# Splitting each 512-column up product of the experts into two products of 256 columns

## The chip, the cores and the metric

The program runs on one core of a Trainium2 chip, in one launch. The metric is the device time of one execution in microseconds (us). TensorE (PE in the rows) multiplies; its weight loads, which bring the stationary operand into the array, have rows of their own (PEld). VectorE is DVE, ScalarE is ACT, GpSimd is POOL, and SyncE (SP) issues nearly all DMAs.

## The reference

Two blocks follow each other, each of two layers over 256 tokens of 1024 features. Only the last part of the second block, a mixture of experts, is touched here:

```
D_MODEL, SEQ, N_EXPERTS, TOP_K, EXPERT_DIM = 1024, 256, 8, 2, 3584

def moe_swiglu(x, w_router, w_gate, w_up, w_down):
    xf = x.reshape(bsz * t, d)
    logits = (xf @ w_router).astype(jnp.float32)
    top_val, top_idx = lax.top_k(logits, TOP_K)
    top_w = jax.nn.softmax(top_val, axis=-1)
    gates = jnp.einsum('nk,nke->ne', top_w, jax.nn.one_hot(top_idx, N_EXPERTS, dtype=jnp.float32))
    out = jnp.zeros_like(xf)
    for e in range(N_EXPERTS):
        h = jax.nn.silu(xf @ w_gate[e]) * (xf @ w_up[e])
        out = out + gates[:, e:e + 1].astype(xf.dtype) * (h @ w_down[e])
    return out.reshape(bsz, t, d)
```

Before it stand the first block (three kinds of attention and an MLP, twice), a gated delta net, a dense SwiGLU of width 2816 (called ffn below) and a window attention.

## The kernel before

All of it is written by hand, engine by engine: in every stage each engine has its own program, its instructions run in the order in which they are written, and engines wait for each other on semaphores.

The part of the experts works on 8 experts of 14 steps each, so 112 steps. A step has 256 hidden columns. Its weights come as three units of 1 MB (128 partitions by 2048 numbers): two "up" units, each with four chunks of 128 input rows and 512 columns (256 of the gate beside 256 of the up matrix), and one "down" unit of two chunks by 1024 columns. That makes 336 units. `moe_order` puts them in order: the two up units of step i, then the down unit of step i - 2 (`LAG`).

Float32 accuracy is made of three products with operands of type float32r. ScalarE rounds a unit into `moe_high` (L3368), VectorE subtracts it from the raw unit to get `moe_low` (L3408), and the tokens of the expert (128 places, gathered) have `moe_xh` and `moe_xl` likewise. TensorE multiplies high by high, high by low and low by high. There are four buffers for split units (`UNITS`), and seven places for raw ones, six in the tile `ring` and one in `xT`. SyncE loads unit u + 7 when VectorE has made unit u's low part (`ring.load`, L3013).

For an up unit the stationary operand is a 128 by 128 block of the tokens, the moving operand one chunk of the unit with its 512 columns, and the result fills one bank of PSUM: gate in columns 0 to 255, up in columns 256 to 511. Four chunks by three kinds of product by two units make 24 products a step (L3312), 2688 in all, which accumulate in one bank for each step. The down products (L3318, 12 a step, 1344 in all) also have 512 columns. After the second up unit of a step TensorE transposes the hidden values of the step before (L3329). ScalarE's SiLU (L3378) and VectorE's product (L3417) read the bank only when all 24 products of the step have ended. At some steps TensorE also gathers tokens for later experts (L3082: moving operand `moe_pick` with 256 columns, stationary blocks of `moe_x_high` or `moe_x_low`) or spreads an expert's result (L3098, L3099: four products of 512 columns in a row with the same stationary block of `moe_pickT`).

Other stages use the same kind of product with 256 moving columns: the ffn's up products (L2023, where the tokens move and 128 by 128 blocks of weights are stationary) and projections (L927).

Of the kernel before, what the change touches and what calls it, by code (L numbers as in the profile page):

```python
# [68 lines left out]
FB = 256  # L69
# [2972 lines left out]
def place(m):  # L3042

    return (0, 1, 0, 2)[m % 4]
# [15 lines left out]
def turn_pick(pe, core, r, m, s, banks):  # L3060

    pick = r["pick"].bitcast(F32)
    for k in range(2):
        for t in range(NT):
            pe.transpose(banks[0][0:CAP, (k * NT + t) * P:(k * NT + t + 1) * P], pick[:, t, k, :], core.const("ident"))
    for k in range(2):
        for t in range(NT):
            mm = pe.matmul(banks[1][0:CAP, k:k + 1], pick[:, t, k, :], r["gates"][:, t, m + k:m + k + 1],
                           start=(t == 0), stop=(t == NT - 1))
    mm.then_inc(s["pick_turned"], 1)  # L3070
# [7 lines left out]
def gather(pe, r, x, chunks, banks):  # L3078

    for n, c in enumerate(chunks):  # L3080
        for t in range(NT):
            mm = pe.matmul(banks[n // 2][:, (n % 2) * 2 * CAP:(n % 2 + 1) * 2 * CAP], x[:, t, c * P:(c + 1) * P],  # L3082
                           r["pick"][:, t, :, :].rearrange("p k n -> p (k n)"), start=(t == 0), stop=(t == NT - 1))
    return mm
# [8 lines left out]
def spread(pe, r, m, t, banks):  # L3093

    for half in range(2):
        cols = slice(half * BANK, (half + 1) * BANK)
        turned = r["pickT"][:, place(m), t * P:(t + 1) * P]
        pe.matmul(banks[half][:], turned, r["yh"][:, cols], start=True, stop=False)  # L3098
        mm = pe.matmul(banks[half][:], turned, r["yl"][:, cols], start=False, stop=True)  # L3099
    return mm  # L3100
# [154 lines left out]
def expert_stage(core, ring, order, r, s):  # L3255
# [3 lines left out]
    high, low, xh, xl, hh, hl, sg = (r[n] for n in ("high", "low", "xh", "xl", "hh", "hl", "sg"))  # L3259
# [10 lines left out]
    def unit(buffers, u):  # L3270
        return unit_of(buffers, ring, u)

    def wait_split(eng, name, u):

        if u >= AHEAD:
            eng.wait_ge(s[name], u - AHEAD + 1)
# [7 lines left out]
    with nc.Block() as block:  # L3284
        @block.sync
        def _(sp):
            for u in range(n_units):
                wait_split(sp, "weight_low", u)
                ring.load(sp, u + len(ring.places))

        @block.tensor
        def _(pe):
            for u, (kind, i, part) in enumerate(order):
                m, own = divmod(i, STEPS)
                wait_split(pe, "weight_high", u)
                if kind == "up" and part == 0 and i >= 2:
                    pe.wait_ge(s["product"], i - 1)
                if kind == "up" and part == 0 and own == 0 and m and m % 2 == 0:
                    pe.wait_ge(s["x_high"], 2 * m)
                    pe.wait_ge(s["x_low"], 2 * m)  # L3300
                if kind == "down":
                    pe.wait_ge(s["hidden_low"], i + 1)
                    if own == 0 and m:
                        pe.wait_ge(s["y_high"], 2 * m)
                        pe.wait_ge(s["y_low"], 2 * m)
                for j, (buffer, other_low) in enumerate(((high, False), (high, True), (low, False))):
                    wt = unit(buffer, u)
                    if j == 2:
                        wait_split(pe, "weight_low", u)
                    if kind == "up":  # L3310
                        for c in range(4):
                            mm = pe.matmul(core.banks[i % 2][:], (xl if other_low else xh)[:, place(m), 4 * part + c, :],  # L3312
                                           wt[:, c, :], start=(part == 0 and j == 0 and c == 0),
                                           stop=(part == 1 and j == 2 and c == 3))
                    else:
                        for half in range(2):
                            for c in range(2):
                                mm = pe.matmul(core.banks[4 + half][:], (hl if other_low else hh)[:, i % 2, c, :],  # L3318
                                               wt[:, c, half * BANK:(half + 1) * BANK],
                                               start=(own == 0 and j == 0 and c == 0),  # L3320
                                               stop=(own == STEPS - 1 and j == 2 and c == 1))
                mm.then_inc(s["unit_used"], 1)
                if u in turn_after:
                    k = turn_after[u]
                    pe.wait_ge(s["product"], k + 1)
                    if k >= 2:
                        pe.wait_ge(s["hidden_low"], k - 1)
                    for c in range(2):
                        mm = pe.transpose(core.banks[2 + k % 2][:, c * CAP:(c + 1) * CAP],  # L3329
                                          sg[:, k % 2, c * P:(c + 1) * P], core.const("ident"))  # L3330
                    mm.then_inc(s["turned"], 1)
                if kind != "up" or part != 1:
                    continue
                if own in SPREAD and m:
                    t = SPREAD.index(own)
                    if t:
                        pe.wait_ge(s["added"], 4 * (m - 1) + 2)
                    else:
                        pe.wait_ge(s["y_high"], 2 * m)
                        pe.wait_ge(s["y_low"], 2 * m)  # L3340
                    spread(pe, r, m - 1, t, core.banks[6:8]).then_inc(s["spread"], 1)
                if own == TURN and m % 2 == 0:
                    pe.wait_ge(s["added"], 4 * m)
                    turn_pick(pe, core, r, m, s, core.banks[6:8])
                if own in GATHER and m % 2:
                    n = GATHER.index(own)
                    pairs = (m - 1) // 2
                    if n == 0:
                        pe.wait_ge(s["picked"], 2 * (pairs + 1))
                        pe.wait_ge(s["added"], 4 * m)  # L3350
                    else:
                        pe.wait_ge(s["x_high"], 4 * pairs + n)
                        pe.wait_ge(s["x_low"], 4 * pairs + n)
                    for rows, bank in ((r["x_high"], 6), (r["x_low"], 7)):
                        gather(pe, r, rows, range(2 * n, 2 * n + 2), core.banks[bank:bank + 1]).then_inc(s["gathered"], 1)
            pe.wait_ge(s["y_high"], 2 * E)
            pe.wait_ge(s["y_low"], 2 * E)
            for t in range(NT):
                spread(pe, r, E - 1, t, core.banks[2 * t:2 * t + 2]).then_inc(s["spread"], 1)
# [310 lines left out]
```

## Time and profile before

| | |
|---|---|
| device time of three runs | 2519.05, 2517.83, 2513.12 us (median 2517.83) |
| span of the profiled execution | 2513.8 us, mean granted TensorE clock 0.985 |
| TensorE busy over the span | 2411.1 us, 96% |
| VectorE, ScalarE busy | 1750.4 us (70%), 1416.7 us (56%) |
| loop over the experts' steps | 1511.3 us to about 2493.7 us of the span |

The profile gives no device time of the profiled execution besides its span, so its own time is taken as 2513.8 us; it lies within the three runs, 4.0 us under their median.

A product's row in the timeline has a start and a duration. Products overlap in the array, so a duration (390 ns for 512 columns) is longer than the distance from one start to the next, and what a product costs in a stream is that distance.

### The profile page before, as it was taken

Reading aid. Unit: us, or ns where it says so; the run is one execution under the profiler, and the core shown is the slowest. Engines: PE = TensorE matmul, PEld = TensorE weight load, DVE = VectorE, ACT = ScalarE, POOL = GpSimd, SP = SyncE. Lnnn points to the kernel's source line nnn. Section 1 sums busy time; section 2 is a strip of 40 time slices with the busy share of each in tenths; the row PEclk is TensorE's granted clock in tenths of the full one; section 3 lists DMA queues with packets and bytes.
Section 4 is the critical chain, followed back from the end, with each engine's and each line's share of the span. In section 5 each row is a group of like instructions: output and inputs, shape, how many; then the busy total and the mean of one; then the engine's idle time right before and its main releaser. Section 6 shows DMA issues by size and latency. Waiting matters only on the chain. (4 is left out here: it accounts for less than half of the span.)

```text
span 2513.8 us, 34646 instructions
## 1 busy us (share of the span) xinstructions
PE 2411.1 (96%) x13815; PEld 2050.2 (82%) x13815; DVE 1750.4 (70%) x2026; ACT 1416.7 (56%) x1624; POOL 136.5 (5%) x176
## 2 busy tenths in 40 slices
PE   6999999999998999998999999999999999999997
PEld 6797789888777898787998888888888888888885
DVE  3357655544676555576545678898899888888987
ACT  4544544453454445433434547777777777777775
POOL 0102200000121000060000000000000000000000
PEclk9999999999999999899999989999999999999998
DMA  8243455533345555405556249999999999999997
GB/s 290 103 140 133 157 188 185 191 135 111 132 151 182 180 198 142 96 1 187 179 188 209 86 134 340 367 366 364 359 363 360 357 354 366 361 356 351 366 362 244
DMA packets 391568, 586.59 MB, mean 233 GB/s; under 512 B 21168, under 2 KB 284656, under 8 KB 391280
## 3 DMA queue, kind: packets, MB, share of 16 engines
q1 hardware_dynamic: 391408, 584.38, 68.7%
q8 instruction: 110, 1.80, 0.3%
q14 instruction: 50, 0.41, 0.1%
HBM read 580.14 MB, written 4.19 MB: 232 GB/s over the span
## 5 line engine op out<-in xcount | busy, mean ns | idle before, releaser
L3408 DVE TENSOR_TENSOR moe_low<-ring,moe_high 128x2048 fp32r<-128x2048 f32 x288 | 658.8, 2290 | 94.2 <-ACT moe_high L3368 90.8
L3368 ACT CAST moe_high<-ring 128x2048 fp32r<-128x2048 f32 x288 | 548.9, 1909 | 143.9 <-PE bank L3312 72.6
L3312 PE MATMUL bank<-moe_high,moe_xh 128*128 128x512 f32 x896 | 243.2, 393 | 1.0 <-PEq L3147 1.0
L3312 PE MATMUL bank<-moe_low,moe_xh 128*128 128x512 f32 x896 | 241.3, 391 | 0.0
L3312 PE MATMUL bank<-moe_high,moe_xl 128*128 128x512 f32 x896 | 240.7, 390 | 0.0
L3312 PEld LDWEIGHTS bank<-moe_high,moe_xh 128*128 128x128 f32 x896 | 168.0, 188 | 38.0 <-issue 1.1
L3312 PEld LDWEIGHTS bank<-moe_high,moe_xl 128*128 128x128 f32 x896 | 168.2, 188 | 37.1
L3312 PEld LDWEIGHTS bank<-moe_low,moe_xh 128*128 128x128 f32 x896 | 168.2, 188 | 37.1
L2079 DVE TENSOR_TENSOR chain_low<-ring,chain_high 128x2048 fp32r<-128x2048 f32 x48 | 110.0, 2292 | 115.7 <-ACT chain_high L2052 115.7
L2052 ACT CAST chain_high<-ring 128x2048 fp32r<-128x2048 f32 x44 | 84.2, 1913 | 139.9 <-PE bank L2023 106.0
L3318 PE MATMUL bank<-moe_high,moe_hh 128*128 128x512 f32 x448 | 128.5, 408 | 0.0
L3318 PE MATMUL bank<-moe_low,moe_hh 128*128 128x512 f32 x448 | 120.6, 391 | 0.0
L3318 PE MATMUL bank<-moe_high,moe_hl 128*128 128x512 f32 x448 | 120.4, 391 | 0.0
L3408 DVE TENSOR_TENSOR moe_low<-xT,moe_high 128x2048 fp32r<-128x2048 f32 x48 | 110.0, 2291 | 13.9 <-ACT moe_high L3368 13.4
L3368 ACT CAST moe_high<-xT 128x2048 fp32r<-128x2048 f32 x48 | 91.6, 1909 | 26.9 <-PE bank L3312 14.0
L2079 DVE TENSOR_TENSOR chain_ffn_low<-ring,chain_ffn_high 128x2048 fp32r<-128x2048 f32 (+1 forms) x34 | 65.0, 1913 | 58.4 <-ACT chain_ffn_high L2052 58.4
L3318 PEld LDWEIGHTS bank<-moe_high,moe_hl 128*128 128x128 f32 x448 | 84.1, 188 | 18.8
L3318 PEld LDWEIGHTS bank<-moe_low,moe_hh 128*128 128x128 f32 x448 | 84.1, 188 | 18.6
L3378 ACT ACTIVATE consts<-bank 128x256 f32<-128x256 f32 x112 | 43.1, 385 | 86.5 <-PE bank L3312 86.5
L2052 ACT CAST chain_ffn_high<-ring 128x2048 fp32r<-128x2048 f32 (+1 forms) x32 | 50.9, 1590 | 66.5 <-PE bank L2023 45.5
L3318 PEld LDWEIGHTS bank<-moe_high,moe_hh 128*128 128x128 f32 x448 | 76.8, 189 | 11.0 <-issue 0.2
L967 DVE TENSOR_TENSOR chain_low<-ring,chain_high 128x1024 fp32r<-128x1024 f32 x36 | 44.0, 1224 | 44.3 <-ACT chain_high L952 35.1
(518 smaller groups left out, 4860.4 us busy)
## 6 DMA issues: line engine op xcount, KB each, us to landing
ring<-in_moe_w_gate SPq DMA_DIRECT2D x199, 512.0 KB, 5.5
ring<-in_moe_w_up SPq DMA_DIRECT2D x199, 512.0 KB, 7.1
ring<-in_moe_w_down SPq DMA_DIRECT2D x95, 1024.0 KB, 7.5
ring<-in_w_in SPq DMA_DIRECT2D x22, 2048.0 KB, 8.1
ring<-in_w_down SPq DMA_DIRECT2D x14, 2048.0 KB, 7.8
ring<-in_w_up SPq DMA_DIRECT2D x10, 2048.0 KB, 8.1
xT<-in_moe_w_down SPq DMA_DIRECT2D x18, 1024.0 KB, 7.5
xT<-in_moe_w_gate SPq DMA_DIRECT2D x31, 512.0 KB, 5.5
```

The lines of the kernel that those rows point to most:

```text
L967: dve.tensor_tensor(unit(core.low, u), raw(u), unit(core.high, u), ALU.subtract)\
L2052: act.copy(unit(core.high, u), raw(u)).then_inc(s["weight_high"], 1)
L2079: dve.tensor_tensor(unit(core.low, u), raw(u), unit(core.high, u), ALU.subtract)\
L3312: mm = pe.matmul(core.banks[i % 2][:], (xl if other_low else xh)[:, place(m), 4 * part + c, :], wt[:, c, :], start=(part == 0 and j == 0 a ...
L3318: mm = pe.matmul(core.banks[4 + half][:], (hl if other_low else hh)[:, i % 2, c, :], wt[:, c, half * BANK:(half + 1) * BANK], start=(own = ...
L3368: act.copy(unit(high, u), ring.raw(u)).then_inc(s["weight_high"], 1)
L3378: act.activation(sg[:, i % 2, :], core.banks[i % 2][:, 0:FB], ACT.Silu).then_inc(s["silu"], 1)
L3408: dve.tensor_tensor(unit(low, u), ring.raw(u), unit(high, u), ALU.subtract)\
```

## The change

Each up product is issued as two: the first multiplies the stationary block by columns 0 to 255 of the chunk into columns 0 to 255 of the bank, the second the same stationary block by columns 256 to 511 into the other half. The flag that begins the accumulation stands on the first of the two alone, at the step's first chunk, and the one that ends it on the second at the step's last chunk. Nothing else changes.

```
--- before.py
+++ after.py
@@ -3309,9 +3309,11 @@
                         wait_split(pe, "weight_low", u)
                     if kind == "up":
                         for c in range(4):
-                            mm = pe.matmul(core.banks[i % 2][:], (xl if other_low else xh)[:, place(m), 4 * part + c, :],
-                                           wt[:, c, :], start=(part == 0 and j == 0 and c == 0),
-                                           stop=(part == 1 and j == 2 and c == 3))
+                            for side in range(2):
+                                cols = slice(side * FB, (side + 1) * FB)
+                                mm = pe.matmul(core.banks[i % 2][:, cols], (xl if other_low else xh)[:, place(m), 4 * part + c, :],
+                                               wt[:, c, cols], start=(part == 0 and j == 0 and c == 0 and side == 0),
+                                               stop=(part == 1 and j == 2 and c == 3 and side == 1))
                     else:
                         for half in range(2):
                             for c in range(2):
```

On TensorE one step with a gather stands in the program before like this (output, moving operand, stationary operand; columns; count):

```order
L3312 MATMUL bank<-moe_high,moe_xh 128x512 x4
L3312 MATMUL bank<-moe_high,moe_xl 128x512 x4
L3312 MATMUL bank<-moe_low,moe_xh 128x512 x4
L3312 MATMUL bank<-moe_high,moe_xh 128x512 x4
L3312 MATMUL bank<-moe_high,moe_xl 128x512 x4
L3312 MATMUL bank<-moe_low,moe_xh 128x512 x4
L3329 MATMUL bank<-consts 128x128 x2
L3082 MATMUL bank<-moe_pick,moe_x_high 128x256 x4
L3082 MATMUL bank<-moe_pick,moe_x_low 128x256 x4
L3318 MATMUL bank<-moe_high,moe_hh 128x512 x4
L3318 MATMUL bank<-moe_high,moe_hl 128x512 x4
L3318 MATMUL bank<-moe_low,moe_hh 128x512 x4
```

At the same place in the changed program TensorE has:

```order
L3314 MATMUL bank<-moe_high,moe_xh 128x256 x8
L3314 MATMUL bank<-moe_high,moe_xl 128x256 x8
L3314 MATMUL bank<-moe_low,moe_xh 128x256 x8
L3314 MATMUL bank<-moe_high,moe_xh 128x256 x8
L3314 MATMUL bank<-moe_high,moe_xl 128x256 x8
L3314 MATMUL bank<-moe_low,moe_xh 128x256 x8
L3331 MATMUL bank<-consts 128x128 x2
L3082 MATMUL bank<-moe_pick,moe_x_high 128x256 x4
L3082 MATMUL bank<-moe_pick,moe_x_low 128x256 x4
L3320 MATMUL bank<-moe_high,moe_hh 128x512 x4
L3320 MATMUL bank<-moe_high,moe_hl 128x512 x4
L3320 MATMUL bank<-moe_low,moe_hh 128x512 x4
```

Every group of four up products has become one of eight with half the columns; order, transposes, gathers and down products stand where they stood, two lines lower in the file.

## Rows read from the trace of the kernel before

**Rows 1.** The page's first part: span, and busy time of each engine.

```profile
span 2513.8 us, 34646 instructions
PE 2411.1 (96%) x13815; PEld 2050.2 (82%) x13815; DVE 1750.4 (70%) x2026; ACT 1416.7 (56%) x1624; POOL 136.5 (5%) x176
```

**Rows 2.** Busy time in one stretch of the experts' loop: its length, engines, clock, DMA.

```profile
1520.00:2490.00 970.00, 970.00 (x4438) 797.08 (x4437) 865.57 (x622) 711.58 (x593) 0.00 (x0) 1.00 1.06 361
```

**Rows 3.** Costliest groups of the page (busy, mean ns, idle before, releaser).

```profile
L3408 DVE TENSOR_TENSOR moe_low<-ring,moe_high 128x2048 fp32r<-128x2048 f32 x288 | 658.8, 2290 | 94.2 <-ACT moe_high L3368 90.8
L3368 ACT CAST moe_high<-ring 128x2048 fp32r<-128x2048 f32 x288 | 548.9, 1909 | 143.9 <-PE bank L3312 72.6
L3312 PE MATMUL bank<-moe_high,moe_xh 128*128 128x512 f32 x896 | 243.2, 393 | 1.0 <-PEq L3147 1.0
```

**Rows 4.** Timeline of the loop, all engines: start us, us, engine, line.

```profile
1995.66 2.29 DVE L3408 TENSOR_TENSOR moe_low<-ring,moe_high 128x2048 fp32r<-128x2048 f32 x1 [0.25 <-ACT moe_high L3368]
...
1998.74 1.91 ACT L3368 CAST moe_high<-ring 128x2048 fp32r<-128x2048 f32 x1 [0.84 <-PE bank L3312]
```

**Rows 5.** DMA in 1520 to 2490 us: queues (packets, MB, share); issues, us to landing.

```profile
q8 instruction: 36, 0.59, 0.3%
...
ring<-in_moe_w_down SPq DMA_DIRECT2D x94, 1024.0 KB, 7.5
```

**Rows 6.** TensorE's timeline in the loop, 512 columns: four steps in a row.

```profile
1608.64 1.09 PE L3312 MATMUL bank<-moe_high,moe_xh 128*128 128x512 f32 x4
...
1614.13 0.38 PE L3329 MATMUL bank<-consts 128*128 128x128 f32 x2
...
1617.11 1.08 PE L3312 MATMUL bank<-moe_high,moe_xh 128*128 128x512 f32 x4
...
1622.63 0.38 PE L3329 MATMUL bank<-consts 128*128 128x128 f32 x2
...
1625.62 1.10 PE L3312 MATMUL bank<-moe_high,moe_xh 128*128 128x512 f32 x4
...
1631.14 0.38 PE L3329 MATMUL bank<-consts 128*128 128x128 f32 x2
...
1634.09 1.07 PE L3312 MATMUL bank<-moe_high,moe_xh 128*128 128x512 f32 x4
...
1635.90 1.07 PE L3312 MATMUL bank<-moe_low,moe_xh 128*128 128x512 f32 x4
1636.81 1.10 PE L3312 MATMUL bank<-moe_high,moe_xh 128*128 128x512 f32 x4
...
1639.58 0.38 PE L3329 MATMUL bank<-consts 128*128 128x128 f32 x2
```

**Rows 7.** TensorE's timeline in the ffn: 96 products of 256 columns.

```profile
1272.94 1.10 PE L2023 MATMUL bank<-x_high,chain_ffn_high 128*128 128x256 f32 x8
1273.88 1.11 PE L2023 MATMUL bank<-x_low,chain_ffn_high 128*128 128x256 f32 x8
...
1275.78 1.07 PE L2023 MATMUL bank<-x_high,chain_ffn_high 128*128 128x256 f32 x8
...
1283.94 0.62 PE L2033 MATMUL bank<-chain_ffn_high,mlp_hh 128*128 128x512 f32 x2
```

**Rows 8.** TensorE's timeline in a projection: 84 products of 256 columns.

```profile
629.82 0.62 PE L927 MATMUL bank<-attention_high,x_high 128*128 128x256 f32 x4
...
639.34 0.38 PE L1461 MATMUL bank<-consts,lower_arena 128*72 128x128 f32 x2
```

**Rows 9.** TensorE's timeline at two gathers inside the experts' loop.

```profile
1684.45 0.62 PE L3082 MATMUL bank<-moe_pick,moe_x_low 128*128 128x256 f32 x4
1684.90 1.08 PE L3318 MATMUL bank<-moe_high,moe_hh 128*128 128x512 f32 x4
...
1702.34 0.64 PE L3082 MATMUL bank<-moe_pick,moe_x_low 128*128 128x256 f32 x4
1702.81 1.09 PE L3318 MATMUL bank<-moe_high,moe_hh 128*128 128x512 f32 x4
```

**Rows 10.** The spreading products' loads and products: duration ns min/median/max.

```profile
L3098 PEld LDWEIGHTS bank<-moe_yh,moe_pickT x32: 186/188/330, 1648.1 to 2497.9; 128*128 128x128 f32 x32
L3098 PE MATMUL bank<-moe_yh,moe_pickT x32: 393/476/628, 1648.2 to 2498.4; 128*128 128x512 f32 x32
```

**Rows 11.** TensorE's timeline at one spread in the loop, stationary block unchanged.

```profile
1648.48 0.40 PE L3099 MATMUL bank<-moe_yl,moe_pickT 128*128 128x512 f32 x1
...
1649.19 1.08 PE L3318 MATMUL bank<-moe_high,moe_hh 128*128 128x512 f32 x4
```

## The prediction, made before the changed kernel was run

> **What bounds the kernel now.** The page's first part shows TensorE busy for 96% of the span [rows 1]. The change touches the experts' loop alone, so the second view is that stretch: in 970 us TensorE is busy for all 970.00, at a granted clock of 1.00, beside VectorE at 865.57 and ScalarE at 711.58 [rows 2]. The costliest groups say who waits for whom: VectorE idles for ScalarE, ScalarE for TensorE (it needs the unit's buffer back), TensorE for nothing but 1.0 us at the loop's entry [rows 3]. So in the loop what sets the time is the distance from one product's start to the next, and the other engines follow.
>
> Two things could stop TensorE from being the limit if its pace changed. Weights: ScalarE's cast at 1998.74 stood idle until TensorE freed the buffer; it lasts 1.91 us, VectorE's subtraction of such a unit 2.29 us [rows 4], and a buffer comes back only every four units, nearly 12 us at about 3 us a unit. That leaves several us between a low part and its first use. DMA: the loop moves 361 GB/s [rows 2], a 1 MB unit lands 7.5 us after its issue [rows 5] and its place is loaded seven units, some 20 us, ahead. I read that as DMA being ahead, since ScalarE's waits name TensorE and no landing [rows 3].
>
> **The change, term by term.** It removes 2688 products of 512 columns and adds 5376 of 256, each with its own load of the stationary block. Nothing moves past anything, no wait is added, no DMA, no work on another engine. The last of the 24 products of a step, for which SiLU waits, becomes two; what both cost is in the term below. So the sum has one term: 2688 times (two paces at 256 columns less one pace at 512).
>
> *The pace at 512 columns.* Four steps in a row, after which the pattern of buffers repeats, have 24 products in 5.49, 5.52, 5.52 and 5.49 us: 22.02 / 96 = 229.4 ns [rows 6]. It isn't one level. The 12 products from 1634.09 to 1636.81 take 2.72 / 12 = 226.7 ns each, the others up to some 231.
>
> *The pace at 256 columns.* The loop has hardly any, but other places have many of the same type, each with a load of its own. In the ffn 96 take 11.00 us, 114.6 ns each; the first 24 of them, right behind products of 512 columns, take 2.84 / 24 = 118.3, and the other 72 take 8.16 / 72 = 113.3 [rows 7]. In a projection 84 take 9.52 us, again 113.3 [rows 8]. Inside the experts' loop, with VectorE, ScalarE and DMA as busy as they will be here, one gather has 0.45 / 4 = 112.5 ns and the next 0.47 / 4 = 117.5 [rows 9]. So there are two levels as well: 113.3 and about 117.5.
>
> The fast level is exactly half of the fast level at 512 (2 x 113.3 = 226.6 against 226.7): time goes by columns, and no fixed cost for a product shows. The slow level costs 8.4 ns a pair more.
>
> *The second load of the same block.* A load is issued for each product even where the block stays: the spreading products have 32 loads for 32 products [rows 10], and three in a row with an unchanged block take 0.71 / 3 = 237 ns [rows 11], near the slow level at 512 and no worse than two slow halves. Loading the same rows again is thus neither skipped nor dear, and at 256 columns the load fits beside the product in 113.3 ns.
>
> *Bounds and value.* All fast: 226.6 - 229.4 = -2.8 ns, -7.5 us. The ffn's mix: 229.2, -0.5 us. Half fast, half slow as in the gathers: 230.8, +3.8 us. All slow: 235.0, +15.1 us (with the ffn's 118.3 it would be +19.4). I take 115.0 ns, four in ten slow, between the ffn's stretch and the gathers, since each step here goes from 512 columns into 48 of 256, as the ffn goes into 96: 230.0 - 229.4 = +0.6 ns, times 2688 = **+1.6 us**. Against the profiled execution that is 2513.8 + 1.6 = 2515.4 us; carried over to the median of the runs, 4.0 us higher, it is 2517.8 + 1.6, about **2519 us**. A measurement of this kernel tells about 0.3% from no change, 7.5 us; the forecast is within it.
>
> A rule speaks against the change: the Trainium skill, "TensorE: Matmul & The Clock Gate", section "Back-to-back issue gap", gives a warm product N / 2.4 ns and a fixed 2.5 ns. By it a pair would cost 2.5 ns more than one product, +6.7 us. The rows of the fast level don't show that fixed part, 226.6 against 226.7.
>
> **Rivals.**
> *Slower, the slow level throughout.* Each up stretch follows products of 512 columns, the ffn's first 24 products behind such were slow [rows 7], and one gather of two never left the slow level [rows 9]. Here the stream switches every 48 products, and each unit begins on another buffer. At 117.5 ns a product: +15.1 us, 2533 us. It decides from a mean of 116.1 ns on (232.2 for a pair, 2.8 above today, 7.5 us). Against it: 72 of 96 in the ffn and all 84 in the projection are fast.
> *A fixed cost for each product.* Rows bound it for a pair between nothing (the fast level) and 235.0 - 229.4 = 5.6 ns (all of the slow level's excess, were it such a cost); the middle, 2.8 ns, is +7.5 us, 2525 us. The fast rows speak against it, the gather at 117.5 ns for it. The skill's fixed part, above, would be this rival.
> *Faster, the fast level throughout.* -7.5 us, 2510 us. For it: the projection, and that today's 512 columns are the ones that lose 2.7 ns to a slow level. It just touches the bound. If the second load were dropped, rows give no more than this, since the columns alone take 0.443 ns each at either width.
> *Code fetch.* TensorE's instructions come in packets: 36 for 4438 products and 4437 loads, if all are its own [rows 2, 5], so 5376 more instructions need some 22 more. A packet takes 0.3% of 970 us x 16 engines / 36 = 1.3 us; were TensorE to stand for each, +28 us, 2546 us. Today it stands for none [rows 2].
> *The change isn't what it says.* The order on TensorE shows eight products of 256 for each four of 512, so it is.
>
> **How the numbers follow.** Mix of levels, as forecast: 0.52. Slow throughout: 0.21. Fixed cost: 0.08. Fast throughout: 0.15. Code fetch: 0.04. Faster by over 0.3% is under half of the fast case, 0.07; slower is slow, fetch, and a little of the fixed cost and the mix's upper end, 0.29; within 0.3% the rest, 0.64. The range goes from the fast end, 2510, to the slow end, 2534; it leaves out the fetch stall and the outer halves of both ends' scatter, under 2 in 10. The likeliest case's own range is 2512 to 2525.
>
> **What would show it.** Right: groups of eight up products start 0.91 to 0.94 us apart; loads as many as products; TensorE busy all 970 us with no new releaser; ScalarE still waits for TensorE; the 12 down products as before. Wrong: up products at 117 ns or more each in most steps (slow rival); holes of about 1 us at regular distances of some 15 us (fetch); a TensorE wait on `moe_high` or `moe_low` (weights late after all); pairs whose second half starts sooner than 110 ns after the first (the load dropped or free). The prediction fails above all if the share of slow products is not that of the ffn, which depends on what stands around them.

## The result: slower by 0.8%, outside the predicted range

| | before | after |
|---|---|---|
| median of the runs | 2518.44 us | 2538.99 us |
| lowest and highest | 2513.12, 2520.42 us | 2534.37, 2540.62 us |
| span of the profiled execution | 2513.8 us | 2537.9 us |

The ratio of after to before is 1.0084, 95% interval 1.0071 to 1.0096. The medians are 20.5 us apart, the spans 24.1 us. Of these 24.1 us, 22.1 lie in the experts' loop, from the start of its first up product to that of its last product (982.0 us before, 1004.1 after). The range had ended at 2534 us, and no change was called likeliest.

The page of the changed kernel, its first part, the queue that carries code, and the three groups that answer to [rows 3]:

```profile
span 2537.9 us, 40022 instructions
...
PE 2435.5 (96%) x16503; PEld 2189.9 (86%) x16503; DVE 1751.7 (69%) x2026; ACT 1416.5 (56%) x1624; POOL 136.5 (5%) x176
...
q8 instruction: 131, 2.15, 0.4%
...
L3410 DVE TENSOR_TENSOR moe_low<-ring,moe_high 128x2048 fp32r<-128x2048 f32 x288 | 659.0, 2291 | 111.6 <-ACT moe_high L3370 106.7
L3370 ACT CAST moe_high<-ring 128x2048 fp32r<-128x2048 f32 x288 | 548.7, 1909 | 152.3 <-PE bank L3314 80.8
L3314 PE MATMUL bank<-moe_high,moe_xh 128*128 128x256 f32 x1792 | 248.8, 281 | 1.0 <-PEq L3147 1.0
```

TensorE's busy time has grown by 24.4 us, as much as the span. VectorE and ScalarE do the same work and idle more, for the same releasers as before. TensorE still waits for nothing but the 1.0 us at the entry. The stretch of [rows 2] in the changed kernel (length; TensorE, its loads, VectorE, ScalarE, GpSimd; clock; DMA share; GB/s):

```profile
1520.00:2490.00 970.00, 970.00 (x6943) 913.75 (x6942) 848.36 (x608) 694.79 (x578) 0.00 (x0) 1.00 1.03 354
```

TensorE is busy for all 970.00 us at the clock of before, and the other engines get less done in the same time (608 instructions on VectorE for 622, 354 GB/s for 361). So nothing stops TensorE: its products themselves come at a slower pace. The timeline of four steps in a row, which answers to [rows 6]:

```profile
1605.08 1.11 PE L3314 MATMUL bank<-moe_high,moe_xh 128*128 128x256 f32 x8
...
1610.78 0.38 PE L3331 MATMUL bank<-consts 128*128 128x128 f32 x2
...
1613.76 1.12 PE L3314 MATMUL bank<-moe_high,moe_xh 128*128 128x256 f32 x8
...
1619.52 0.38 PE L3331 MATMUL bank<-consts 128*128 128x128 f32 x2
...
1622.50 1.07 PE L3314 MATMUL bank<-moe_high,moe_xh 128*128 128x256 f32 x8
...
1625.22 1.12 PE L3314 MATMUL bank<-moe_high,moe_xh 128*128 128x256 f32 x8
...
1628.10 0.38 PE L3331 MATMUL bank<-consts 128*128 128x128 f32 x2
...
1631.08 1.11 PE L3314 MATMUL bank<-moe_high,moe_xh 128*128 128x256 f32 x8
...
1636.74 0.38 PE L3331 MATMUL bank<-consts 128*128 128x128 f32 x2
```

The four steps take 5.70, 5.76, 5.60 and 5.66 us, together 22.72 us for 192 products: 118.3 ns each, 236.7 for a pair against 229.4 before. That is +7.3 ns, and times 2688 it is +19.6 us, nearly the whole loss between the medians (20.5). Over the whole loop, added up in the trace from the start of each of the 224 up units to the start of what follows it, the up products take 616.3 us before and 637.7 us after, +21.4 us; the down products take 317.4 and 318.1 us.

There are three levels (a level is a pace that a stream of products holds), not the two that the prediction knew, and they go with the buffer of the weights. Units take the four buffers in turn, so these eight up units use buffers 3, 0, 2, 3, 1, 2, 0 and 1. Buffers 2 and 3 go at 120.0 ns (5.76 / 48 from 1613.76; 2.88 / 24 from 1625.22). Buffers 0 and 1 go at 117.9 (5.66 / 48 from 1631.08), once at 113.3 (2.72 / 24 from 1622.50). In the whole loop the 111 units in buffers 2 and 3 all settle at 120, and of the 113 units in buffers 0 and 1, 99 settle at 118 and 14 at 113. No row used for the prediction was above 118.3.

### The profile page after: what moved, and what is told of

It is laid out like the page before. It is cut to its first block and busy times, and to the rows that moved or that the text cites. A ratio compares the mean times of both kernels' runs of the same rounds, so it can differ in the third digit from the quotient of the medians.

```text
span 2537.9 us, 40022 instructions
## 1 busy us (share of the span) xinstructions
PE 2435.5 (96%) x16503; PEld 2189.9 (86%) x16503; DVE 1751.7 (69%) x2026; ACT 1416.5 (56%) x1624; POOL 136.5 (5%) x176
## 5 line engine op out<-in xcount | busy, mean ns | idle before, releaser
L3314 PE MATMUL bank<-moe_high,moe_xh 128*128 128x256 f32 x1792 | 248.8, 281 | 1.0 <-PEq L3147 1.0
L3314 PE MATMUL bank<-moe_low,moe_xh 128*128 128x256 f32 x1792 | 249.2, 281 | 0.0
L3314 PE MATMUL bank<-moe_high,moe_xl 128*128 128x256 f32 x1792 | 249.0, 281 | 0.0
L3314 PEld LDWEIGHTS bank<-moe_high,moe_xh 128*128 128x128 f32 x1792 | 235.6, 189 | 10.0 <-issue 1.1
L3314 PEld LDWEIGHTS bank<-moe_low,moe_xh 128*128 128x128 f32 x1792 | 228.5, 190 | 0.0
L3314 PEld LDWEIGHTS bank<-moe_high,moe_xl 128*128 128x128 f32 x1792 | 228.4, 190 | 0.0
```

What stands on the lines that cost most here:

```text
L3314: mm = pe.matmul(core.banks[i % 2][:, cols], (xl if other_low else xh)[:, place(m), 4 * part + c, :], wt[:, c, cols], start=(part == 0 and ...
```

## The experiments

Two theories stood at first. By A the loss is in what the split adds, the same block loaded twice in a row or halves of a bank that change with every product. By B it is in what the products read, since the levels differ by buffer and not by order. "The kernel" below is the changed one where not said otherwise; ratios are to the kernel before, with the 95% interval behind them.

**The halves in another order.** The first four products of a group go to one half, the next four to the other, so no block is loaded twice in a row and the half changes once:

```
...
-                        for c in range(4):
-                            for side in range(2):
+                        for side in range(2):
+                            for c in range(4):
...
```

> As the changed kernel, 5376 up products of 256 columns, but the four chunks run inside the two halves: no stationary block is loaded twice in a row, and the half of the bank stays for four products. Theory A (the second load of the block just loaded, or the change of half in the bank, costs some 5 ns a product): the mean distance of up products falls from 118.6 ns to 113 to 115 ns, the time to about 2512 to 2520 us, ratio to the kernel before 0.997 to 1.002. Theory B (any product of 256 columns with its own load costs this here, whatever the order): distance 118 to 120 ns, time about 2539 us, ratio 1.007 to 1.010.

Measured: 2541.81 us, ratio 1.0087 [1.0057, 1.0117], with the levels of the changed kernel, unit for unit (120 in buffers 2 and 3, 118 and 14 times 113 in the others); the up products add up to 637.7 us as there.

**Halves change, blocks don't repeat.**

```
...
+                        for turn in range(2):
+                            for c in range(4):
+                                side = (c + turn) % 2
...
```

> As the run before, but the halves of the bank alternate from product to product while the stationary block is another each time. If repeated loading of one block is the cost (theory A1): about 113 to 115 ns a product, ratio 0.997 to 1.002. If the alternation of the halves is the cost (theory A2), or theory B: 118 to 120 ns, ratio 1.007 to 1.010.

Measured: 2539.37 us, ratio 1.0082 [1.0054, 1.0111]. The same levels again, 638.0 us of up products.

**Blocks repeat, halves don't change.** The block of `moe_xh` is loaded for the high part and again for the low part, into one half:

```
...
+                    for side in range(2):
+                        cols = slice(side * FB, (side + 1) * FB)
+                        for c in range(4):
+                            for wt in (wh, wl):
+                                pe.matmul(bank[:, cols], xh[:, place(m), 4 * part + c, :], wt[:, c, cols],
...
```

> Products of 256 columns; the block of the tokens' high part is loaded twice in a row, for the unit's high and then its low part, and both products go into the same half of the bank; a third of the products (the tokens' low part) have another block each time. Theory A1 (repeated block costs): the first two thirds stay at 118 to 120 ns, the last third falls to about 113 ns, ratio about 1.005. Theory A2 (alternation costs): all at 113 to 115 ns, ratio 0.997 to 1.002. Theory B: all at 118 to 120 ns, ratio 1.007 to 1.010.

Measured: 2540.57 us, ratio 1.0087 [1.0057, 1.0116]. Its up products take 638.0 us. Four orders, with the repeated load or without and with the halves changing or not, give 1.0082 to 1.0087 and the same time of up products within 0.3 us. Theory A falls. The second load of a block costs what any load costs. A small kernel that was to run these orders with TensorE alone gave no result.

**The addresses alone.** What differs between buffers 0 and 1 and buffers 2 and 3 is where they lie: in the program's address map, in bytes within a partition and modulo 256 (the residue), the first two are at 224 and the other two at 160, as are the tokens' blocks `moe_xh` and `moe_xl`. No trace shows an address. That the blocks and buffers 2 and 3 agree follows from the sizes of the tiles between them, all multiples of 256 bytes; the 224 is the author's reading of the map, and the runs with gaps below bear it out. A small kernel of its own has streams of 96 products of 256 columns and of 24 of 512, with stationary tiles at 160 and 224 and moving tiles at each multiple of 32:

```
STAT = {"stat_e": 224, "stat_c": 160}
MOVE = {"mov_a": 0, "mov_b": 32, "mov_c": 64, "mov_d": 96, "mov_e": 128, "mov_f": 160, "mov_g": 192, "mov_h": 224}
...
                for x in STAT:
                    for w in MOVE:
                        narrow(pe, banks[0][:], stat[x], move[w])
                        wide(pe, banks[1][:], stat[x], move[w])
```

> A small kernel with none of the reference's computation. TensorE alone runs, for two stationary tiles (address 224 and 160 modulo 256, as the blocks of weights in the ffn and the experts' tokens have it) and eight moving tiles (addresses 0, 32, ... 224 modulo 256), 96 products of 256 columns and then 24 of 512; then four of these pairs again beside ScalarE's casts and VectorE's subtractions. In the experts' loop moving buffers at 160 (as the tokens) stood at 120.0 ns, those at 224 at 116.7 to 118. Theory C (the load and the moving reads collide by address): with equal residues 120 ns, with others 113.3 or 117.7, alone as well as beside the others. Theory D (the other engines' traffic does it): 113.3 throughout while TensorE is alone, 117 to 120 beside them. Theory E (a phase that the stream happens to lock into): levels of 113.3 and 117.7 without order by address, perhaps changing inside a group or kept from the group before.

Its timeline on TensorE (moving, stationary operand), the streams at the distances 64, 192 and 0 for the one stationary tile and then for the other:

```profile
65.38 11.04 PE L23 MATMUL bank<-mov_b,stat_e 128*128 128x256 f32 x96
76.25 5.66 PE L31 MATMUL bank<-mov_b,stat_e 128*128 128x512 f32 x24
...
132.87 11.06 PE L23 MATMUL bank<-mov_f,stat_e 128*128 128x256 f32 x96
143.76 5.76 PE L31 MATMUL bank<-mov_f,stat_e 128*128 128x512 f32 x24
...
166.31 11.67 PE L23 MATMUL bank<-mov_h,stat_e 128*128 128x256 f32 x96
177.82 5.63 PE L31 MATMUL bank<-mov_h,stat_e 128*128 128x512 f32 x24
183.28 11.67 PE L23 MATMUL bank<-mov_a,stat_c 128*128 128x256 f32 x96
...
267.84 11.67 PE L23 MATMUL bank<-mov_f,stat_c 128*128 128x256 f32 x96
279.35 5.63 PE L31 MATMUL bank<-mov_f,stat_c 128*128 128x512 f32 x24
284.82 11.36 PE L23 MATMUL bank<-mov_g,stat_c 128*128 128x256 f32 x96
...
301.62 11.04 PE L23 MATMUL bank<-mov_h,stat_c 128*128 128x256 f32 x96
312.50 5.66 PE L31 MATMUL bank<-mov_h,stat_c 128*128 128x512 f32 x24
317.99 0.22 PE L88 MATMUL bank<-stat_c 128*128 128x128 f32 x1
```

A stream's pace is the distance to the next stream's start over its count. With both operands at the same residue the 96 narrow products take 11.51 us (119.9 ns), for `stat_e` from 166.31 as for `stat_c` from 267.84. At 64 apart they take 10.87 and 10.88 us (113.3), from 65.38 and 301.62. So the single addresses don't matter, and the distance from the stationary to the moving operand does. By the sizes of its tiles the two pairs at distance 0 lie 66048 and 45312 bytes apart, which are 0 and 256 modulo 512, and they have the same pace, so a period of 512 isn't seen. All of them, as (start to start) / count, mean of the two tiles:

| moving less stationary, mod 256 | 0 | 32 | 64 | 96 | 128 | 160 | 192 | 224 |
|---|---|---|---|---|---|---|---|---|
| 256 columns, ns | 119.9 | 116.7 | 113.3 | 119.9 | 120.0 | 117.4 | 113.4 | 118.3 |
| 512 columns, ns | 227.7 | 233.5 | 229.0 | 233.8 | 232.9 | 234.2 | 233.3 | 232.9 |

For 256 columns the distances 0, 96 and 128 are the slowest, for 512 distance 0 is the fastest. Theory C of the expectation had 120 at distance 0 alone: it holds there, but 96 and 128 are as slow. The other engines were idle, so D falls. In a second part of that kernel, with ScalarE and VectorE working as in the loop, the streams at distances 0, 64 and 192 gave the same paces but for one: 64 apart, 256 columns took 117.8 instead of 113.3, both times right behind 512-column products at distance 0.

This sorts the rows that the prediction had read. By the address map, in the ffn the tokens move (160) and weights stand (224), and the gathers have moving `moe_pick` at 160 and stationary `moe_x_high` at 224: distance 192, one of the two at which 113.3 occurs. The experts' up products have 0 in half of their units and 64 in the other half, which none of those rows had.

**The kernel with the tokens' blocks moved to 224.** Unused gaps of 64 and 192 bytes a partition between tiles make the distances 0 for buffers 0 and 1 and 192 for buffers 2 and 3. This is how all gaps below are made, with other sizes:

```
...
+            gap = {"xh": 64, "hh": 192}.get(name, 0)
+            if gap:
+                memory.enter_context(nc.sbuf_tensor(f"moe_gap_{name}", [P, gap // 4], F32))
...
```

> The changed kernel, with an unused gap of 64 bytes ahead of the tokens' blocks (moe_xh, moe_xl) and one of 192 behind them, so that these lie at 224 modulo 256 and nothing else changes its residue. Theory C (the pace of a stream goes by the distance of moving and stationary address modulo 256; small kernel: 0 gives 120 ns, 64 gives 113.3 or 117.8, 192 gives 113.5): the levels of the units change places, units in buffers 2 and 3 (distance 192) fall from 120 to 113.5 ns, units in buffers 0 and 1 (distance 0) rise from 117.5 to 120; mean 116.7, up products 10 us cheaper than in the changed kernel, ratio to the kernel before 1.003 to 1.006. Theory F (it is the experts' loop itself, or its weights' buffers, that is slow at 256 columns): levels stay, ratio 1.007 to 1.010.

Measured: 2540.73 us, ratio 1.0089 [1.0071, 1.0107]. By time alone this is the other theory's range (1.007 to 1.010), but the levels changed places. A unit in buffer 1 and then one in buffer 2:

```profile
1663.40 1.10 PE L3314 MATMUL bank<-moe_high,moe_xh 128*128 128x256 f32 x8
...
1666.26 1.09 PE L3314 MATMUL bank<-moe_high,moe_xh 128*128 128x256 f32 x8
...
1669.00 0.38 PE L3331 MATMUL bank<-consts 128*128 128x128 f32 x2
```

The first takes 2.86 / 24 = 119.2 ns, the second 2.74 / 24 = 114.2, slow in its first products and at 113 in the rest. All 113 units in buffers 0 and 1 now settle at 120; of the 111 in buffers 2 and 3, 21 settle at 113 and 90 at 118. That the levels follow the distance is shown in the kernel itself. The forecast missed in that it had all units at distance 192 on the fast level.

**All up products at distance 192** (gaps `{"xh": 128, "hh": 192, "pick": 192}` and 64 bytes ahead of weight buffers 2 and 3; the down products, of 512 columns, are then at distance 0):

> The changed kernel, with gaps so that all four pairs of weight buffers lie at 224 modulo 256, the tokens' blocks at 32 (distance 192 for all up products of 256 columns) and the hidden blocks at 224 (distance 0 for the down products of 512). Theory C: up products 113.5 ns, 227.0 for two against 229.4 for one of the kernel before, 6.5 us less; down products 226.7 to 227.9 against 229.4, 2 to 3.6 us less; together ratio 0.995 to 0.998. Theory F: about 118 ns as in the changed kernel, ratio 1.006 to 1.010.

Measured: 2532.36 us, ratio 1.0057 [1.0043, 1.0071]. A step in its timeline:

```profile
1653.78 1.11 PE L3314 MATMUL bank<-moe_high,moe_xh 128*128 128x256 f32 x8
...
1659.43 0.38 PE L3331 MATMUL bank<-consts 128*128 128x128 f32 x2
```

5.65 / 48 = 117.7 ns, and 220 of the 224 up units settle at 118: the 120.0 is gone, the 113.3 didn't come, and the time lies above both the 0.995 to 0.998 of the theory and the kernel before.

**The kernel before, all at distance 0** (unsplit; gaps `{"xh": 64, "pick": 192}` and the 64 bytes):

> The kernel before, unsplit, with gaps so that weight buffers, the tokens' blocks and the hidden blocks all lie at 224 modulo 256 (distance 0 for all products of 512 columns). Theory C: 226.7 to 227.9 ns a product against 229.4, 4032 products, 6 to 11 us less, ratio 0.9955 to 0.998. Theory F: as the kernel before, ratio 0.999 to 1.001.

Measured: 2509.62 us, ratio 0.9967 [0.9953, 0.9981]. It is faster than both kernels of this study. Its timeline has 107 of the 112 steps of 24 products at 226.8 to 227.1 ns, where [rows 6] had 229.4:

```profile
1652.97 1.07 PE L3312 MATMUL bank<-moe_high,moe_xh 128*128 128x512 f32 x4
...
1658.42 0.38 PE L3329 MATMUL bank<-consts 128*128 128x128 f32 x2
...
1661.36 1.07 PE L3312 MATMUL bank<-moe_high,moe_xh 128*128 128x512 f32 x4
...
1666.80 0.38 PE L3329 MATMUL bank<-consts 128*128 128x128 f32 x2
```

**The kernel before, distances 160 and 96** (unsplit; gaps `{"xh": 160, "hh": 96}`):

> The kernel before, unsplit, with the tokens' blocks at 64 modulo 256, so that up products of 512 columns have distances 160 (buffers 0 and 1) and 96 (buffers 2 and 3). Theory C: 234.3 and 233.4 ns as in the small kernel, 233.9 against 229.4, some 12 us more, ratio 1.004 to 1.006. Theory F: ratio 0.999 to 1.001.

Measured: 2527.89 us, ratio 1.004 [1.0025, 1.0054]. A step in its timeline:

```profile
1663.21 1.09 PE L3312 MATMUL bank<-moe_high,moe_xh 128*128 128x512 f32 x4
...
1668.83 0.38 PE L3329 MATMUL bank<-consts 128*128 128x128 f32 x2
```

5.62 / 24 = 234.2 ns, and all but two of its up units take 232.7 to 234.8. Addresses alone move the unsplit kernel by 18.3 us (2527.89 - 2509.62).

**The split at those same addresses.** The gaps of the two kernels above, in the changed kernel; first distance 0:

> The changed kernel at the addresses of the run with everything at 224 modulo 256 (distance 0), so that it differs from that run by the split alone. Theory C: 120.0 ns a product, 240.0 for two against 226.7 for one, 13.3 ns times 2688 = 36 us above that run (2509.6 us), 2545 us, ratio to the kernel before 1.010 to 1.013. Theory F (the loop is slow at 256 columns by some 118.6 ns whatever the addresses): 1.005 to 1.008.

Measured: 2548.11 us, ratio 1.0116 [1.0097, 1.0136], as theory C of the expectation had it, 120.0 ns in nearly all units:

```profile
1655.72 1.12 PE L3314 MATMUL bank<-moe_high,moe_xh 128*128 128x256 f32 x8
...
1661.47 0.38 PE L3331 MATMUL bank<-consts 128*128 128x128 f32 x2
```

Then distances 160 and 96:

> The changed kernel with the tokens' blocks at 64 modulo 256 (distances 160 and 96), to be set beside the unsplit run at the same addresses (ratio 1.004). Theory C, by the small kernel's 117.3 and 120.0 ns: 234.6 against 234.3 in buffers 0 and 1, 240.0 against 233.5 in buffers 2 and 3, on average 3.4 ns times 2688 = 9 us above the unsplit run, ratio to the kernel before 1.006 to 1.009: here the split costs less than half of what it costs at the addresses of the kernel before.

Measured: 2543.75 us, ratio 1.0107 [1.0083, 1.0131], above the 1.006 to 1.009 expected. One unit at distance 160 and the next at 96:

```profile
1661.80 1.10 PE L3314 MATMUL bank<-moe_high,moe_xh 128*128 128x256 f32 x8
...
1664.62 1.12 PE L3314 MATMUL bank<-moe_high,moe_xh 128*128 128x256 f32 x8
...
1667.50 0.38 PE L3331 MATMUL bank<-consts 128*128 128x128 f32 x2
```

96 gives 120.0 as it should (2.88 / 24). 160 gives the small kernel's 117.4 in some units, as here (2.82 / 24 = 117.5), and 118.6 to 118.8 in most, 118.5 in the mean. The cost of one and the same edit is thus 38.5 us at distance 0 (2548.11 - 2509.62), 20.5 at the kernel's own mix of 0 and 64, and 15.9 at 160 and 96 (2543.75 - 2527.89). The first and the last are differences between two sets of runs; by the ratios they are 37 and 17 us, each uncertain by some 6 or 7 us, so by time alone the last two costs can't be told apart. The traces can: the up products take 34.6 us more at distance 0 (609.9, then 644.5), 21.4 more at the mix, 12.8 more at 160 and 96 (628.3, then 641.1).

**What picks 113.3 or 117.7.** Two theories for distances 192 and 64: by G the stream has two levels there, and keeps the one on which it enters; by H the loop's traffic or waits cost the 4 ns. First, the down products split too, all at distance 192 (gaps `{"xh": 128, "pick": 128}` and the 64 bytes):

```
...
+                                for side in range(2):
+                                    cols, at = slice(side * FB, (side + 1) * FB), half * BANK + side * FB
...
```

> Up and down products both of 256 columns (8064 in all), all at distance 192; besides gathers, spreads and transposes TensorE runs one width. Theory G (at distances 64 and 192 a stream has two stable levels, 113.3 and 117.7 ns, and stays at the one in which it was entered; a stream of 512 columns hands over the slow one): mostly 113.3 ns, ratio 0.996 to 1.001. Theory H (the traffic or the waits of the loop hold it at 117.7 ns): 117.7 for all, 235.4 for two against 229.4 for one, 4032 times 6 ns = 24 us more, ratio 1.008 to 1.011.

Measured: 2529.9 us, ratio 1.0051 [1.0033, 1.0068], between the ranges of both theories. Its timeline has both levels, 5.45 / 48 = 113.5 ns in one step and 5.66 / 48 = 117.9 in the next:

```profile
1658.15 1.07 PE L3314 MATMUL bank<-moe_high,moe_xh 128*128 128x256 f32 x8
...
1663.60 0.38 PE L3333 MATMUL bank<-consts 128*128 128x128 f32 x2
...
1666.65 1.10 PE L3314 MATMUL bank<-moe_high,moe_xh 128*128 128x256 f32 x8
...
1672.31 0.38 PE L3333 MATMUL bank<-consts 128*128 128x128 f32 x2
```

A step keeps its level to its end, as G has it, under the same traffic. The whole loop says so: 140 of its 336 units are fast and 196 slow, none changes its level inside, and neither does the stream at any of the 222 places where an up unit follows a unit with nothing between. It changes where something stands between: across a step's transposes (with or without a gather or a spread) it fell 38 times, rose 39 times and stayed 33 times. So G is right on the keeping and wrong on "mostly 113.3".

Then TensorE alone, with the loop's sequences of 12, 48 and 2 products at distances 192, 64 and 0, and 288 in a row (a small kernel again):

> A small kernel with none of the reference's computation and TensorE alone: 48 products of 256 columns at distance 192, six times (a) one after another, (b) each behind 12 products of 512 columns, (c) each behind two transposes and these 12, as in the loop; (d) and (e) as c at distance 64 and 0; (f) as b with the ffn's roles, moving tile at 160, blocks at 224. Theory G: a and f 113.3 ns, b or c 117.7 ns as in the loop, d 117.7, e 120. Theory H: a, b, c, d and f all 113.3 after a few products, e 120.

Its timeline, the 288 and then two of the sequences at distance 192, below them one at distance 64, and last one with the ffn's roles:

```profile
30.28 34.08 PE L32 MATMUL bank<-mov_h,stat_a 128*128 128x256 f32 x288
64.20 2.91 PE L23 MATMUL bank<-mov_h,stat_h 128*128 128x512 f32 x12
66.94 5.82 PE L32 MATMUL bank<-mov_h,stat_a 128*128 128x256 f32 x48
72.60 2.91 PE L23 MATMUL bank<-mov_h,stat_h 128*128 128x512 f32 x12
...
169.36 5.82 PE L32 MATMUL bank<-mov_h,stat_c 128*128 128x256 f32 x48
175.01 0.38 PE L38 MATMUL bank<-ident,rawb 128*128 128x128 f32 x2
...
281.67 5.82 PE L32 MATMUL bank<-mov_f,stat_e 128*128 128x256 f32 x48
287.32 2.88 PE L23 MATMUL bank<-mov_h,stat_h 128*128 128x512 f32 x12
```

33.92 / 288 = 117.8 ns and 5.66 / 48 = 117.9, with no other engine at work, and 5.65 / 48 = 117.7 at distance 64: H falls, since the slower level needs no traffic. Part of G's forecast missed as well. It had the 288 and the ffn's roles at 113.3, and both stayed at 117.8.

What picks the level on entry stays open in the main, but the traces show one half of it: behind 512-column products at distance 0 the fast level was never taken. Here all streams at 192 and 64 stand behind such products and all are slow. So are the two at 64 in the second part of the first small kernel, where those at 64 and 192 behind products at other distances were fast. In the changed kernel none of the 27 units at distance 64 right behind a down unit at distance 0 is fast, and 12 of the 27 behind a down unit at distance 64 are. With all up products at 192, the down products had been put at distance 0, and none of the 109 up units right behind them is fast. Another distance ahead is no promise of the fast level, as the other 15 units show.

## Why the prediction was wrong

**The step that failed is the pace at 256 columns**, "I take 115.0 ns, four in ten slow, between the ffn's stretch and the gathers". The loop has 118.3. Pairs cost 236.7 ns for 229.4, +19.6 us, where the sum had 230.0 and +1.6 us. The rows it was taken from [rows 7 to 9] are right, but the ffn and the gathers read operands 192 apart, where 113.3 is possible. The loop reads them 0 and 64 apart. At 0 there is no such level: 119.9 in the small kernel, 120.0 in the loop. At 64 there is, but 99 of 113 units were slow, where the prediction had four in ten. The prediction had asked what stands around the stream; it should have asked first what the stream reads, which says what levels there are, and then what stands ahead.

**The share of slow products was read from one stretch of the ffn.** The first ffn stretch of the kernel before, of the same products, is slow to its end:

```profile
1195.88 1.10 PE L2023 MATMUL bank<-x_high,chain_ffn_low 128*128 128x256 f32 x8
...
1217.55 0.63 PE L2033 MATMUL bank<-chain_ffn_high,mlp_hh 128*128 128x512 f32 x2
```

That is 184 products in 21.67 us, 117.8 ns each. And in the stretch of [rows 7] the level changed neither with the time since the 512 columns nor by itself: 16 products were slow, then the 18th started 164 ns behind the 17th, and from there on the pace was the fast one. The 118.3 of "the first 24" holds this hole. That the 48 products of a step, without such a hole, would fall to the fast level as the ffn's 96 did was therefore not to be had from these rows.

**The loss in two parts.** Added up over the loop, the units at distance 0 take 304.6 us before and 319.3 after, +14.7 us, 11.0 ns a pair. Those at distance 64 take 311.7 and 318.5, +6.8 us, 5.0 ns a pair. At distance 0 the split would cost 13.3 ns (240.0 for 226.7) if all the unsplit units were on their fast level, but 512 columns have two levels there as well, one for each buffer in [rows 6]:

```profile
1611.41 1.07 PE L3312 MATMUL bank<-moe_high,moe_xh 128*128 128x512 f32 x4
```

The unit in buffer 2 from 1608.64 to this row takes 2.77 / 12 = 230.8 ns, the one in buffer 3 from here to 1614.13 takes 226.7. In the loop before, 44 of the 55 up units in buffer 2 settle at 231 and all 56 in buffer 3 at 227. With all up products at distance 0 the 224 units all settle at 227; what picks this level wasn't looked into.

**The step from "the fast level is exactly half"** to "no fixed cost for a product shows" held for the rows read, and for no general rule: 2 x 113.3 against 226.7 compares a distance of 192 with one of 0. At one and the same distance the split costs 12.1 ns at 0 (2 x 119.9 - 227.7), and gains 2.4 at 64 and 6.5 at 192 where the small kernel was on the fast level. On the slow level, 117.8, it costs 6.6 at 64 and 2.3 at 192.

**The rivals.** "Slow throughout" was nearest: it named the right sign, the place (up products at 117 ns or more in most steps), and the point from which it decides (116.1). Its price of +15.1 us was too small, since it took 117.5 as the worst level. A fixed cost isn't what happened, since the cost hangs on the addresses. By the rule of the Trainium skill, "TensorE: Matmul & The Clock Gate", section "Back-to-back issue gap", which gives the fixed 2.5 ns for an isolated product, a pair would pay an estimated 2.5 ns, +6.7 us; the runs have 15.9 to 38.5 us by the addresses, so the measurement decides against it here. Code fetch: the page of the profile has 131 packets, and 110 before, 21 more where some 22 were worked out, and TensorE stands for none of them.

**What held.** The second load of the same block is neither skipped nor dear: four orders give the same time. Weights and DMA stay ahead: TensorE waits for nothing in the loop. No wait of note changed its releaser. The split is what the order showed.

**What stays open.** Why the distance matters isn't shown. That the reads of a load and of the product beside it meet in the memory at some distances would fit, but no run looked inside. Distances that aren't multiples of 32 bytes were not tried, nor other widths. That 160 gave 118.6 to 118.8 in most units of the kernel and 117.4 alone wasn't followed further. What picks the level is known only in the half said above; 64 gave 113.3 and 117.8 with TensorE alone, so the other engines aren't needed for it.

## What to carry to other kernels

When the pace of TensorE's stream is the bound, a pace read elsewhere in the same kernel carries over only if the operands lie alike: compare the addresses of the moving and the stationary tile modulo 256 before using it. For streams of this type keep 512 columns with both at the same residue, which two or three unused gaps of 64 to 192 bytes can give: 0.33% of this kernel (0.19 to 0.47) for no instruction. A pace with more than one level needs more than one stretch to read it from. An edit whose price hangs on the layout should be tried at more than one layout before it is called good or bad.

## What the runs showed of the hardware

The distance from one float32r product to the next, each with its own load, depends on (moving less stationary address) modulo 256: 113.3 to 120.0 ns at 256 columns, 226.7 to 234.2 at 512. Distance 0 is among the slowest at 256 columns (119.9) and the fastest at 512 (227.7). At distances 64 and 192 products of 256 columns have two levels, 113.3 and about 117.8, and one level can last through 288 products (in the loop with all products split, none of 336 units changed its level inside). At distance 0 products of 512 columns have two levels as well, 226.7 and about 231. Loading the same block again costs the same as loading another one (637.7 to 638.0 us of up products in four orders).
